# Recurrence of a hybrid flow trunk: the next tile's preparation is spread between the current tile's Gram blocks and solve levels

## The reference, cut to what matters

```python
def _rwkv_scan(S0, r, w, kk, a, k, v, reverse):
    def step(S, inp):
        r_t, w_t, kk_t, a_t, k_t, v_t = inp
        sa = jnp.einsum('bhvk,bhk->bhv', S, -kk_t)
        S = S * w_t[:, :, None, :] + sa[..., None] * (kk_t * a_t)[:, :, None, :] + v_t[..., None] * k_t[:, :, None, :]
        return S, jnp.einsum('bhvk,bhk->bhv', S, r_t)
...
w_logit = (p['rwkv_w0'] + jnp.einsum('btdr,drc->btdc', jnp.tanh(wl), p['rwkv_w2'])).astype(f32)
decay = jnp.exp(-jnp.exp(-jax.nn.softplus(-w_logit) - 0.5))
a = jax.nn.sigmoid((p['rwkv_a0'] + jnp.einsum('btdr,drc->btdc', al, p['rwkv_a2'])).astype(f32))
kk = kk * lax.rsqrt(jnp.sum(kk * kk, -1, keepdims=True) + 1e-12)
k_h = heads(k[:, :, None, :] * (1.0 + (a - 1.0) * p['rwkv_k_a'])).astype(f32)
for d in range(2):
    S, o = _rwkv_scan(state0[:, d], rh, w_h[:, :, d], kk, a_h[:, :, d], k_h[:, :, d], vh, reverse=(d == 1))
# then: sum of both directions, group norm per head, bonus term, gate
```

## Time and profile before

| | |
|---|---|
| median of 3 runs | 2866.76 us (2860.07 to 2869.19) |
| the profiled execution | 2869.25 us, of which the span of the trace is 2865.3 us |
| granted PE clock, mean over the span | 0.935 of full speed |
| PE busy | 2600.9 us (91%), 23158 matmul instructions |
| DVE, ACT, POOL busy | 1426.4 us (50%), 1061.8 us (37%), 325.4 us (11%) |
| the recurrence's four tiles, first layer | 813.5 to 1034.0 us, then the last scan |
| the same, second layer | from 2223.2 us |

### The profile page before, as it was taken

One profiled execution on the slowest core, in us unless ns is written; L12 is line 12 of the kernel. 1 busy time (PEld: TensorE's weight loads), 2 busy tenths in 40 slices (PEclk: granted clock), 3 DMA queues, 4 the chain that ended last, 5 costly groups with the idle time before them and its releaser, 6 DMA issues. The chain is left out here.

```text
span 2865.3 us, 56276 instructions
## 1 busy us (share of the span) xinstructions
PE 2600.9 (91%) x23158; PEld 2405.5 (84%) x23158; DVE 1426.4 (50%) x2319; ACT 1061.8 (37%) x1713; POOL 325.4 (11%) x316
## 2 busy tenths in 40 slices
PE   5999999999678888999979999989996888899998
PEld 3889998888667878999968898988785788799997
DVE  3333466545666546443353335655365655454434
ACT  3333244344533324432253323443354333243323
POOL 0000121000032213100100002300000223040001
PEclk7999999998789998999989999999897899989999
DMA  8766433232100012446466663432221000134463
GB/s 270 240 212 204 152 102 108 81 92 65 59 2 3 3 43 82 126 127 192 125 214 214 227 189 113 121 95 79 79 74 38 3 3 25 50 95 126 125 204 107
DMA packets 482184, 319.92 MB, mean 112 GB/s; under 512 B 15474, under 2 KB 438920, under 8 KB 481800
## 3 DMA queue, kind: packets, MB, share of 16 engines
q1 hardware_dynamic: 481928, 316.32, 36.3%
HBM read 311.30 MB, written 4.98 MB: 110 GB/s over the span
## 5 line engine op out<-in xcount | busy, mean ns | idle before, releaser
L828 PE MATMUL acc<-xm_hi,w_hi 128*128 128x384 f32 x2512 | 875.0, 348 | 54.1 <-DVE xm_lo L2005 33.1
L830 PE MATMUL acc<-xm_hi,w_lo 128*128 128x384 f32 x2512 | 857.0, 341 | 0.0
L829 PE MATMUL acc<-xm_lo,w_hi 128*128 128x384 f32 x2448 | 834.1, 341 | 0.0
L1995 DVE TENSOR_TENSOR w_lo<-raw,w_hi 128x1024 fp32r<-128x1024 f32 (+1 forms) x420 | 521.6, 1242 | 495.8 <-ACT w_hi L1471 488.3
L828 PEld LDWEIGHTS acc<-xm_hi,w_hi 128*128 128x128 f32 x2512 | 486.1, 194 | 98.0 <-issue 57.8
L1471 ACT ACTIVATE w_hi<-raw 128x1024 fp32r<-128x1024 f32 (+1 forms) x420 | 438.7, 1044 | 306.9 <-PE acc L830 226.4
L830 PEld LDWEIGHTS acc<-xm_hi,w_lo 128*128 128x128 f32 x2512 | 484.8, 193 | 0.0
L829 PEld LDWEIGHTS acc<-xm_lo,w_hi 128*128 128x128 f32 x2448 | 471.9, 193 | 1.5
L828 PE MATMUL acc<-h_hi,w_hi 128*128 128x384 f32 x704 | 243.1, 345 | 8.7 <-DVE w_lo L1995 8.7
L829 PE MATMUL acc<-h_lo,w_hi 128*128 128x384 f32 x704 | 240.2, 341 | 0.0
L830 PE MATMUL acc<-h_hi,w_lo 128*128 128x384 f32 x704 | 240.1, 341 | 0.0
(11 more groups left out here) (338 smaller groups left out, 3387.9 us busy)
## 6 DMA issues: line engine op xcount, KB each, us to landing
raw<-in_ffn_w_in SPq DMA_DIRECT2D x179, 512.0 KB, 3.9
modw<-in_w_mod SPq DMA_DIRECT2D x71, 1024.0 KB, 6.1
raw<-in_w_in SPq DMA_DIRECT2D x114, 512.0 KB, 4.1
raw<-in_ffn_w_out SPq DMA_DIRECT2D x64, 512.0 KB, 4.8
raw<-in_ffn_w_out SPq DMA_DIRECT2D x32, 384.0 KB, 3.5
raw<-in_w_up SPq DMA_DIRECT2D x24, 512.0 KB, 3.5
modx<-in_w_mod SPq DMA_DIRECT2D x9, 1024.0 KB, 13.0
raw<-in_w_out SPq DMA_DIRECT2D x16, 512.0 KB, 4.2
```

The costliest lines, as they stand in the source:

```text
L828: pe.matmul(out, lhs[0], rhs[0], start=first, stop=False)
L829: pe.matmul(out, lhs[0], rhs[1], start=False, stop=False)
L830: return pe.matmul(out, lhs[1], rhs[0], start=False, stop=last)
L1995: done(dve.tensor_tensor(w_lo[:, c % SPL, 0:w], raw[:, c % RAW, 0:w], w_hi[:, c % SPL, 0:w].bitcast(F32), ALU.subtract), lo_done)
```

## The change

PE may now make a tile's decay products behind Gram blocks 0 and 1 (in bank `acc3`), and its rate products in level 2 (banks `acc1` and `acc0`). The old tile's scan steps 2 and 3 stand in levels 1 and 2, its norm in levels 3 to 5. `cs`, `zi` and `half` have a buffer for each direction, `zx` is gone (its values overwrite `sg` or `cs`). `prepare_sums` is split into `sum_decays` (the scan instruction) and `centre_sums` (the three that follow), `prepare_exps` into four functions, so that they stand at different places. `key_factor` takes the tanh itself (factor and bias are halved in `small`), so ACT no longer waits for POOL's `rate`, which now waits for `key_factor`. `lam`, `eps` and `half` share one tile.

```diff
-                half = sb("half", [128, NQ], ctx=ph)
+                cs = sb("cs", [128, 2, TOK], ctx=ph)
+                zi = sb("zi", [128, 2, TOK], ctx=ph)
-            link(dve.tensor_scalar(small[:, 8:12], par[:, 155:159], -1.0, 1.0, ALU.mult, ALU.add))
+            link(dve.tensor_scalar(small[:, 8:12], par[:, 155:159], -0.5, 1.0, ALU.mult, ALU.add))
+            link(dve.tensor_scalar(small[:, 12:16], par[:, 155:159], 0.5, None, ALU.mult))
...
@@ PE
+                    def prepare_decay(j, d):
+                        if j == 0:
+                            bank = pb[2 + d]
+                        else:
+                            bank = acc[3]
+                            if d == 1:
+                                pe.wait_ge(decay_done, 2 * j + 1)
+                            elif j >= 3:
+                                pe.wait_ge(out_done, j - 2)
...
                         gram(j, 0)
                         if old:
                             scan_right(s, 0)
+                        if nxt:
+                            prepare_decay(j + 1, 0)
                         gram(j, 1)
                         if old:
                             scan_solve(s, 0)
+                        if nxt:
+                            prepare_decay(j + 1, 1)
                         gram(j, 2)
...
+                        level_xlx(j, 1, 0)
+                        if old:
+                            scan_update(s, 2)
+                        level_xlx(j, 1, 1)
+                        if old:
+                            scan_right(s, 3)
+                        if nxt:
+                            prepare_rate(j + 1, 0)
+                        level_lx(j, 2, 0)
+                        level_lx(j, 2, 1)
...
                             level_xlx(j, n, 0)
+                            if old and n == 4:
+                                tile_var(s)
+                            if old and n == 5:
+                                tile_root(s)
                             level_xlx(j, n, 1)
@@ ACT
+                    def key_factor(g):
+                        j, d = g // 2, g % 2
+                        done(act.activation(kt[:, d, :], aa[:, d, :], ACT.Identity, scale=small[:, 12 + j:13 + j],
+                                            bias=small[:, 8 + j:9 + j]), key_part)
@@ POOL
                     def rate(g):
-                        pool.wait_ge(rate_done, g + 1)
-                        done(pool.tensor_scalar(aa[:, g % 2, :], aa[:, g % 2, :], 0.5, 0.5, ALU.mult, ALU.add), aa_ready)
+                        d = g % 2
+                        pool.wait_ge(key_part, g + 1)
+                        link(pool.tensor_scalar(aa[:, d, :], aa[:, d, :], 0.5, 0.5, ALU.mult, ALU.add))
...
+                        if nxt:
+                            decay(2 * j + 2)
+                            decay(2 * j + 3)
                         for n in range(1, NL + 1):
                             mask(j, n, 0)
                             mask(j, n, 1)
...
                             if n == 3 and nxt:
                                 rate(2 * j + 2)
                                 rate(2 * j + 3)
+                            if n == 4 and nxt:
+                                keys(2 * j + 2)
@@ DVE
                         first_level(j, 1)
                         if old:
+                            scan_solve(s, 1)
+                        if nxt:
+                            sum_decays(g0)
+                        first_level_done(j, 1)
+                        if old:
+                            scan_state(s, 1)
+                        if nxt:
+                            centre_sums(g0)
...
+                        level_add(j, 2, 0)
+                        if nxt:
+                            centre_sums(g1)
+                        level_add(j, 2, 1)
+                        if nxt:
+                            prepare_norm(j + 1)
+                        if old:
+                            tile_centre(s)
+                        level_add(j, 3, 0)
+                        if nxt:
+                            prepare_keys(g0)
+                            prepare_keys(g1)
+                        level_add(j, 3, 1)
+                        if nxt:
+                            prepare_queries(g0)
+                        level_add(j, 4, 0)
+                        if nxt:
+                            prepare_decayed(g0)
+                        level_add(j, 4, 1)
+                        if nxt:
+                            prepare_queries(g1)
+                        if old:
+                            tile_root(s)
+                        scan_start(j)
+                        level_add(j, 5, 0)
+                        if old:
+                            tile_norm(s)
+                        level_add(j, 5, 1)
+                        if nxt:
+                            prepare_decayed(g1)
                         if old:
                             tile_out(s)
```

More of the change, by code:

```diff
@@ L1164, in prepare_norm, with prepare_rate @@
                         if j >= 1:
-                            pe.wait_ge(rate_done, 2 * j + 2)
+                            pe.wait_ge(rate_done, 2 * j + 1)
                         expand(acc[1] if j >= 1 else pb[1], rn, 2 * j).then_inc(rn_t, 1)
[L1168 to L1183, removed]
+                    def prepare_decay(j, d):
[7 more added lines that the diff above has]
+                                pe.wait_ge(out_done, j - 2)
+                        pe.matmul(bank[:, 0:TOK], lora_w[HALVES[d], j * 128:(j + 1) * 128], cmix[HALVES[d], 12, :],
+                                  start=True, stop=True).then_inc(lora_decay, 1)
+                    def prepare_rate(j, d):
+                        if j == 0:
+                            pe.wait_ge(decay_done, d + 1)
+                        bank = pb[2 + d] if j == 0 else acc[1 - d]
+                        pe.matmul(bank[:, 0:TOK], lora_a[HALVES[d], j * 128:(j + 1) * 128], cmix[HALVES[d], 13, :],
+                                  start=True, stop=True).then_inc(lora_rate, 1)
                     def gram(j, p):
@@ L1712, in level_lx @@
                                        ), tl_ready)
-                    def key_factor(g):
-                        j, d = g // 2, g % 2
-                        act.wait_ge(aa_ready, g + 1)
-                        done(act.activation(kt[:, d, :], aa[:, g % 2, :], ACT.Identity, scale=par[:, 155 + j:156 + j],
-                                            bias=small[:, 8 + j:9 + j]), key_part)
                     def scan_right(j, i):
@@ L1768, in _ @@
                         key_factor(g)
-                        prepare_exps(g)
+                    for g in range(2):
+                        exp_reads(g)
+                        exp_writes(g)
+                        exp_keys(g)
+                        exp_halves(g)
                     for j in range(NB):
                         nxt, old = j + 1 < NB, j >= 1
-                        s = j - 1
+                        s, g0, g1 = j - 1, 2 * j + 2, 2 * j + 3
                         gram(j, 0)
@@ L1779, in _ @@
                         gram(j, 3)
+                        copy_tok(j, 0, 1)
                         if old:
@@ L1822, in _ @@
+                        if old:
+                            tile_affine(s)
                             tile_high(s)
@@ L1959, in _ @@
                         rate(g)
-                    for g in range(2):
                         keys(g)
@@ L1966, in _ @@
                             mask(j, n, 1)
-                            if n == 2 and nxt:
-                                decay(2 * j + 2)
-                                decay(2 * j + 3)
                             if n == 3 and nxt:
@@ L2430, in _ @@
                     for g in range(2):
-                        prepare_sums(g)
+                        sum_decays(g)
+                        centre_sums(g)
+                    for g in range(2):
                         prepare_keys(g)
+                    for g in range(2):
                         prepare_queries(g)
@@ L2452, in _ @@
                         if old:
-                            scan_state(s, 1)
+                            tile_bonus(s)
                         gram(j, 5)
```

234 lines of the change are left out of this document (109 added, 125 removed).

## The result

The changed kernel takes 2845.43 us (median of 5 runs, 2841.49 to 2846.58), the kernel before in the same rounds 2866.76; the ratio is 0.9928, 95% interval 0.991 to 0.9946. So it is faster by 0.7%, and 21 us were gained where 40.6 had been forecast. From the last product ahead of a layer's recurrence to the last spread of the root, 252.3 us in both layers before, it is 242.1 in the first layer and 243.4 in the second: 10.1 and 8.9 less, where 20.3 had been forecast for each.

The account below looks back on a forecast made before the run. A full tile is bound by PE, with holes, mainly the seam. Per layer 9.6 + 4.5 + 4.5 + 1.7 = 20.3 us, both layers 40.6: 2828.6 from the profiled 2869.25, 2826 as median; range 2815 to 2837.

Parts of the forecast that it names:

- The seam: Between tiles: PE's idle time for `kt` and the slow clock behind it go; seam and first blocks 8.5 us less.
- Tile 3: A layer's last tile, which prepares nothing: 1.7 us of slow clock and 0.7 gained, 0.7 lost; gain 1.7.
- tile 0's: A layer's first tile: end 4.0 us earlier, its seam gains 6.4, less 0.8 of restarts; gain 9.6.
- Starts some 1.5 later: Tile 0's first block comes 1.5 us later, since both directions' sums and keys stand before the first queries.
- Come without a wait and at full clock: Tile 0's second-direction blocks, which waited 2.99 us before, come without a wait and at full clock.
- Lose 1.7 by the same inserts: Tile 0's levels, 20.70 us before, lose 1.7 to preparation work inserted between the directions' sums.
- The decay products: Tile 0's levels gain 1.3 us because these products are made earlier.
- The walk through a full tile: Tiles 1 and 2: 47.0 us of PE work, 7.0 of waits, 1.1 of restarts; 55.1 against 59.6, gain 4.5 each.
- Rival 1: Fills give most back: inserts beside POOL in levels 2 to 5 cost 18 us more, 2844; chance 0.16.
- Rival 2: The clock falls in the levels behind two waits of each tile; six tiles lose 20 us, 2846; chance 0.10.
- Rivals 3 and 4: 3: preparation fully on the levels' path, 2887, chance 0.04. 4: PE still waits for `kt` at seams, about 2866, 0.04.

Follow-up runs that it names:

- the two kernels that differ in the unread products alone: Changed kernel with nothing of the next tile between a level's two sums, 2826.34 us; the same plus 19 rate products nobody reads in the layer-start wait, 2820.12 us.
- the kernel with the lowest time: Changed kernel with nothing of the next tile between a level's two sums and 19 rate products nobody reads at a layer's start: 2820.12 us.
- all five kernels with unread products: Rate products nobody reads added: changed kernel 34 (2850.36 us), 17 (2843.65), 19 with sums edit (2820.12), 13 with sums and start edits (2823.01); kernel before 13 (2867.56).
- the kernel before with unread products: Kernel before the change plus 13 rate products nobody reads in its 9.3 us wait at a layer's start: 2867.56 us, ratio 0.9998.

## Why the prediction was right in its mechanism and wrong in its size

**The seam** held. No `kt` wait but the first of a layer, the clock at 1.00 behind the seams of tiles 1 and 2. From update to update (870.18, 926.10, 980.83) the periods are 55.9 and 54.7; 55.1 had been forecast, and 59.6 before. **Tile 3** gained 3.2 and not 1.7, from the update in it to the next one: 49.45 before (989.86 to 1039.31), 46.25 now (980.83 to 1027.08). These three give 11.8 against the forecast's 10.7.

**The step that failed is tile 0's**: 9.6 us had been forecast and 1.7 were lost, from the last product before the recurrence (803.0 and 801.0) to the first update (870.59 and 870.18). That is 11.3 us of the first layer, and all of its miss: the measured 2845 lies outside the forecast's own range of 2815 to 2837. Its terms:

- "Starts some 1.5 later": 2.9. Of the 1.4 more, 1.34 is GpSimd beside VectorE, by the run with its products cut. The forecast had counted the order of the work but not that `rate` and `keys` of GpSimd now run just beside it.
- "Come without a wait and at full clock": they came without a wait and at half clock. The forecast charged nothing for the clock here. In the kernel before it was low for 3.2 us behind the first wait and for 3.4 near the second; here it stayed low for 10.4. Price 4.15, by the two kernels that differ in the unread products alone.
- "Lose 1.7 by the same inserts": 3.8, by the run without them, with the slow stretch behind level 5's wait. Another 2.1. The decayed pair, put at 1.6, took 2.4 in each of tiles 0 to 2 (1.14 and 1.23); the keys, put at 1.8, took 1.8 and 1.6.
- The decay products were credited where they left the levels (1.3), and not charged where they now stand, ahead of level 2: 2 x 0.84 at full clock. This and some 2 us that I can't assign are read off the walk and were not tried by themselves; even the kernel with the lowest time begins level 2 at 32.6 us from the last product, where the forecast had 29.1. Besides the start and the decay products, a rate product of 0.84 stands ahead of it there.

**The walk through a full tile** had the right sum with wrong parts. Tile 1's waits in levels 3, 4 and 5 are 0.31, 1.52 and 1.63 (0.75, 1.75 and 1.05 forecast), the start's is 1.08 (0.8), those of step 2 and of the root do not show. Their sum is 4.5 for 7.0.

**Rival 1** (the fills give most of it back) named 2844, and that this is the time is luck. It put 18 us on top of what the forecast had charged for the inserts, 1.7 in tile 0 and 0.75 + 1.75 + 1.05 in each of tiles 1 and 2, together 8.8 us a layer. The run without them gives 3.8 + 2.9 + 2.1 = 8.8 in these tiles of the first layer: they cost what had been charged, too little in tile 0 and too much in the others. That this run takes 2826.3, the forecast's number, is chance as well: it pays for no inserts, but for the start and the clock. **Rival 2** (the clock in the levels) is true of the waits of 2.2 to 2.5 in nearly all tiles 0, and of some of those of 1.2 to 1.6. The forecast had argued against it by one row of a full tile, and in the changed kernel the clock fell in this way once in a layer, not behind two waits of each tile, as the 2846 supposes. The Trainium skill ("TensorE: Matmul & The Clock Gate", A second HAM failure mode: psum-queue depth-cycling) has short idles between groups of matmuls make the clock swing; this trace agrees in part, since waits of 1.26 and 1.24 were followed by 1.00 in one layer and by 0.68 in the other. **Rivals 3 and 4** fell.

## What to carry to other kernels

Where an engine waits for the second of two sums, work that is moved under them belongs behind the pair, not between them: the place cost 18 us here, nearly what the whole change had brought. A wait for several things hides the next one, so price each by taking it away. And when a stall moves, walk through what follows it at the clock that the stall leaves, not at the clock of the kernel before.

## What the runs showed of the hardware

- The same stretch of TensorE work took 47.7 and 43.5 us in the two layers of one execution, with waits of 1.24 and 1.26 us ahead of it: the clock behind a wait of 1.2 to 1.6 us is not settled by its length alone.
- VectorE operations with two inputs in SBUF and GpSimd operations take turns; what one costs beside the other depends on which begins first. At a layer's start in the changed kernel, on both engines:

```profile
810.20 0.56 DVE L2367 SCALAR_TENSOR_TENSOR ar<-kk,sg 128x384 f32<-128x384 f32 x1
810.80 1.23 DVE L2369 TENSOR_TENSOR ar<-cmix,cs 128x384 f32<-128x384 f32 x1
```

```profile
810.25 1.37 POOL L1987 TENSOR_TENSOR aa<-aa,kk 128x384 f32<-128x384 f32 x1
```

  The first VectorE row begins 0.05 ahead of GpSimd's and takes its usual 0.56. The second begins beside it and ends 0.41 behind its end (811.62). It is so in both layers' recurrences of the changed kernel: all 48 such operations of 384 columns that began while a GpSimd one ran ended 0.40 to 0.42 behind its end, and took from 0.64 to 1.24; all 30 that began first took their usual time. GpSimd's product is stretched likewise: 1.37 here behind the first row, and 0.99 at 809.85 in the kernel before, where VectorE waits. The Trainium skill ("SBUF — State Buffer", Terms) says that the two share a port pair and that the loser fully blocks. The trace agrees: the wait of 0.82 and a whole 0.56 would make 1.38, and the 1.23 is shorter by the same 0.15 as in the other rows. So what an insert costs beside GpSimd is set by the order in which the two begin, not by a price between 0.56 and 1.23, as the forecast took it.
- In tile 3 PE stood idle once for 0.3 to 2.0 us where the profile names no releaser, in at least one layer of all five kernels with unread products (0.5 to 2.0) and of four of the others (0.3 to 0.8). In the kernel before with unread products the clock fell behind it (tile 3 79.4 in one layer, 74.7 in the other, which has no such idle time). Its cause was not tried.
